# A four-layer transformer stack on one core: modulation pieces one unit later, the angle table inside a feed-forward stage, the closing x update shared with GpSimd, output by feature halves

## The chip, the cores and the metric

One core of one Trainium2 chip runs the whole program. Its engines are TensorE (PE, with its weight loads PEld), VectorE (DVE), ScalarE (ACT), GpSimd (POOL) and the sync engine's DMA queue (SP). The metric is the device time of one execution in microseconds. Everything is float32.

## The reference

x is 512 positions by 1024 features. Two blocks follow each other, each with two layers. A layer of the first block is a mixing part and a gated feed-forward part; a layer of the second block is a hybrid mixer and a feed-forward part with squared ReLU:

```python
for l in range(DEPTH):                                   # first block
    mod = c_act @ w_mod[l] + b_mod[l]                    # six vectors of 1024
    sh1, sc1, g1, sh2, sc2, g2 = split(mod)
    h = _rms(x, ln1[l]) * (1 + sc1) + sh1
    x = x + g1 * _mixing(h, ...)                         # top-k, stick-breaking and window attention
    h = _rms(x, ln2[l]) * (1 + sc2) + sh2
    x = x + g2 * ((silu(h @ w_gate) * (h @ w_up)) @ w_down)
for l in range(DEPTH):                                   # second block
    mod = cond @ w_ada[l] + b_ada[l]
    h = rmsnorm(x, norm_g[l, 0]) * (1 + sc_m) + sh_m
    y = hybrid(h, cos, sin, ...)                         # differential attention, latent attention, state scan
    x = x + g_m * rmsnorm(y, norm_g[l, 1])
    h = rmsnorm(x, norm_g[l, 2]) * (1 + sc_f) + sh_f
    y = square(relu(h @ w_up)) @ w_down
    x = x + g_f * rmsnorm(y, norm_g[l, 3])
```

cos and sin of the second block come from an input of positions, so the kernel computes that table of angles itself.

## The kernel before

**Layout.** x is kept in SBUF turned, as `xT`: eight tiles of 128 features by 512 positions. `hT` holds the normalized input. Weights come in slabs of up to 2 MB through a ring of two slots, `ring`; the sync queue issues slab n when the last product on slab n - 2 is done. Products go to eight PSUM banks.

**Order.** There is no scheduler. `order1(l)` and `order2(l)` write out one list of steps for each layer (`STEPS1`, `STEPS2`), and every engine walks the same list and does its part of each step, with semaphores between the parts. So a step's place in the list sets its place in the queue of each engine that has a part in it. `woven(*streams)` merges streams of steps: each is given a start and an end on a common scale, its steps are spread evenly between, and all are sorted by that position.

**Feed-forward stages.** `FFN1` has 38 units, `FFN2` 32. A unit is one product of two-by-two block form with seven part products (L1037): "gu" units make the hidden tiles, "dn" units the output, where two units (the second closes) make one result. Two units share a slab. For each unit GpSimd forms sums of weight blocks (`slab_sums`, step "S", L928 to L933, four additions, two units ahead), ScalarE copies the first product (L1518), VectorE recombines the products (L1998 to L2010) and, in the second block, forms the block differences of the hidden tiles ("turn", L1969 to L1972). `first_pair` (L1082) does the first two units of a stage together.

**Modulation of the next layer.** It is computed within a feed-forward stage from 24 pieces of 256 columns. The step "ma" is VectorE's weighted sum over half a piece (`mod_sum`: one instruction of L1958 and three of L1960 each), "mm" is TensorE's sum over partitions (`mod_product`, L1022), "mb" adds the bias. `ffn_steps` puts ma 2t and 2t + 1 behind unit t, mm t - 1 behind unit t, and mb t - 2 ahead of it. The half pieces are loaded by the sync queue (L874) between the slabs (L882), as `pieces_behind` says; half piece p is issued only when the sum of p - 2 is done. This happens in three of the four feed-forward stages.

**Ends of layers.** The second block starts with the steps prep, ns, nh: VectorE prepares small vectors, ScalarE squares the eight tiles of x (L1767), TensorE sums them with a matrix of ones (L1325), ScalarE forms the root, VectorE and ScalarE make `hT` (L2358, L1776). Ahead of it, behind the last step of the first block, VectorE computes the angle table in 18 small instructions (L2268 to L2279) and ScalarE its sine (L1716). A layer of the second block ends with "ys" (ScalarE squares the output y, L1738, GpSimd adds the squares, L981), "post" (TensorE's sum, ScalarE's root) and the x update on VectorE: for each of eight tiles y = y * modG * rb (L2557), x = x + y (L2558). After the last layer TensorE turns x back (L1505), VectorE copies eight banks (L2563), and one transfer of 2 MB writes the output (L900):

```python
            pe.wait_ge(*s2["x"].after(DEPTH - 1, KT))
            for i in range(QT):
                for half in range(2):
                    b = 2 * i + half
                    pe.wait_ge(free[b], final[b])
                    for t in range(4):
                        mm = pe.transpose(bank[b][:, P * t:P * t + P], xT[:, 4 * half + t, P * i:P * i + P], ident)
```

**Woven stages.** In the first block the top-k selection is 48 rounds of two VectorE instructions (L2157, L2158), woven with projections ("pj", "proj", "pss", "rope") and with the eight window groups, whose last step but one, "on", is VectorE's normalization (L2254) and whose last, "ot", is TensorE's turn of the result (L1281). In the second block 32 scans (L2528) are woven with the projections, the rotations "kr" and "mqr" (TensorE L1365, VectorE L2372) and the outputs "y" (L1478); the gated norms "sn" (L1359) and the output projection "wo" are woven with the attention groups.

## Time and profile before

| what | value |
|---|---|
| median of 3 runs | 3379.56 us (3372.46 to 3388.6) |
| profiled execution | 3382.9 us, its span 3381.1 us |
| busy: PE, PEld | 3074.4 us (91%), 2214.9 us (66%) |
| busy: DVE, ACT, POOL | 1730.5 us (51%), 761.5 us (23%), 923.7 us (27%) |
| mean granted TensorE clock | 0.941 |
| read from memory | 300.6 MB, 90 GB/s over the span |
| chain that ended last | PE 75%, DVE 12%, ACT 5%, DMA 2%, POOL 2% |

In the rows further down a line of a timeline is start, length, engine, source line, operation, tiles, shapes and count; brackets give how long the engine was idle before it and what it waited for. Merged lines of TensorE count each float32 product twice.

### The profile page before, as it was taken

The numbers are of one execution on the slowest core, as the hardware profiler recorded it, in microseconds if no ns is written. First come the engines' busy times: TensorE is split into PE (matmuls) and PEld (weight loads), VectorE is DVE, ScalarE is ACT, GpSimd is POOL, SyncE is SP. The second block draws the span as 40 slices with busy tenths as digits, with TensorE's granted clock in tenths as the row PEclk, the third lists the DMA queues.
The fourth block names the chain that finished last, engine by engine and source line by source line (L and its number), as shares of the span: only waits on it lengthen the run. The fifth ranks groups of instructions, "written<-read, shape, count | busy, mean of one in ns | idle before, by whom it ended". The sixth has DMA issues, their size and how long they took to land.

```text
span 3381.1 us, 34673 instructions
## 1 busy us (share of the span) xinstructions
PE 3074.4 (91%) x12632; PEld 2214.9 (66%) x12632; DVE 1730.5 (51%) x3718; ACT 761.5 (23%) x1781; POOL 923.7 (27%) x796
## 2 busy tenths in 40 slices
PE   6988989999998798999979988799997998899996
PEld 3444568888744467888854355688883435588885
DVE  1384337785328644877542633775724353452333
ACT  2234420000123542000022243310202234320110
POOL 0220023344312012344410400343440120234442
PEclk8997899999999889999989989899998998899998
DMA  5113214442211002445121111244421010122221
GB/s 203 62 39 146 79 63 162 172 169 98 95 50 50 25 13 93 165 155 196 62 77 45 34 49 38 87 150 185 164 100 46 33 50 26 50 75 75 100 75 50
DMA packets 38553, 304.97 MB, mean 90 GB/s; under 512 B 4192, under 2 KB 4320, under 8 KB 24176
## 3 DMA queue, kind: packets, MB, share of 16 engines
q1 hardware_dynamic: 38352, 302.68, 24.6%
q8 instruction: 103, 1.69, 0.2%
q14 instruction: 66, 0.54, 0.1%
q0 software_dynamic: 32, 0.07, 0.0%
HBM read 300.63 MB, written 2.10 MB: 90 GB/s over the span
## 4 chain that ended last, share of the span: by engine, by line
PE 75%; DVE 12%; ACT 5%; issue 3%; DMA 2%; POOL 2%; DVEq 0%; SPq 0%; POOLq 0%; ACTq 0%
PE bank L1037 41%; PE bank L1015 9%; PE bank L1345 7%; PE bank L1166 3%; PE bank L1082 3%; DMA ring<-in_slabs 2%; DVE nw L1960 1%; DVE sel L2158 1%; PE bank L1216 1%; DVE m L2157 1%; PE bank L1478 1%; PE bank L1153 1%; DVE SPT L2222 1%; PE bank L1203 1%; PE bank L1325 1%
## 5 line engine op out<-in xcount | busy, mean ns | idle before, releaser
L928 POOL TENSOR_TENSOR SPT<-ring 128x512 f32<-128x512 f32 (+2 forms) x140 | 170.4, 1217 | 1023.7 <-DMA ring<-in_slabs 501.9
L1037 PE MATMUL bank<-U,ring 128*128 128x256 f32 x1728 | 406.5, 380 | 0.3 <-DMA ring<-in_slabs 0.3
L1037 PEld LDWEIGHTS bank<-U,ring 128*128 128x128 f32 x1728 | 326.3, 190 | 43.6 <-DMA ring<-in_slabs 0.4
L1960 DVE SCALAR_TENSOR_TENSOR nw<-sel,c,nw 128x256 f32<-128x256 f32 x504 | 321.3, 638 | 40.3 <-DMA sel<-in_mod_pieces 22.7
L1037 PE MATMUL bank<-U,SPT 128*128 128x256 f32 x1296 | 311.4, 379 | 4.9 <-POOL SPT L933 4.9
L1037 PEld LDWEIGHTS bank<-U,SPT 128*128 128x128 f32 x1296 | 246.0, 190 | 39.4 <-POOL SPT L933 6.1
L1037 PE MATMUL bank<-hT,SPT 128*128 128x256 f32 x1088 | 257.0, 379 | 0.0
L1037 PE MATMUL bank<-hT,ring 128*128 128x256 f32 x1088 | 256.1, 389 | 0.3 <-DMA ring<-in_slabs 0.3
L1345 PE MATMUL bank<-hT,ring 128*128 128x512 f32 x544 | 246.0, 597 | 6.5 <-ACT hT L1776 6.5
L1166 PE MATMUL bank<-hT,ring 128*128 128x512 f32 x512 | 243.9, 620 | 5.0 <-ACT hT L1559 3.2
L1998 DVE TENSOR_TENSOR rb<-bank,nw 128x256 f32<-128x256 f32 x108 | 45.8, 424 | 375.8 <-PE bank L1037 286.4
L1037 PEld LDWEIGHTS bank<-hT,ring 128*128 128x128 f32 x1088 | 207.8, 195 | 27.9 <-DMA ring<-in_slabs 0.3
L1037 PEld LDWEIGHTS bank<-hT,SPT 128*128 128x128 f32 x1088 | 206.7, 190 | 28.1
L1518 ACT ACTIVATE nw<-bank 128x256 f32<-128x256 f32 x108 | 40.7, 377 | 759.4 <-PE bank L1037 759.0
L931 POOL TENSOR_TENSOR SPT<-SPT,ring 128x512 f32<-128x512 f32 (+2 forms) x140 | 190.1, 1358 | 0.0
L1015 PE MATMUL bank<-U,ring 128*128 128x512 f32 (+2 forms) x416 | 185.8, 588 | 0.0
L1345 PEld LDWEIGHTS bank<-hT,ring 128*128 128x128 f32 x544 | 99.8, 190 | 127.1 <-issue 124.1
L1166 PEld LDWEIGHTS bank<-hT,ring 128*128 128x128 f32 x512 | 99.0, 199 | 126.5 <-issue 124.5
L930 POOL TENSOR_TENSOR ring<-ring 128x512 f32<-128x512 f32 (+2 forms) x140 | 176.6, 1261 | 11.0
L933 POOL TENSOR_TENSOR SPT<-ring,SPT 128x512 f32<-128x512 f32 (+2 forms) x140 | 173.8, 1241 | 11.0
L990 POOL TENSOR_TENSOR SPT<-SPT,U 128x512 f32<-128x512 f32 (+3 forms) x48 | 55.9, 1190 | 332.2 <-DVE SPT L2528 332.2
L1015 PEld LDWEIGHTS bank<-U,ring 128*128 128x128 f32 (+1 forms) x416 | 84.1, 210 | 79.9 <-issue 76.6
(328 smaller groups left out, 4735.8 us busy)
## 6 DMA issues: line engine op xcount, KB each, us to landing
ring<-in_slabs SPq DMA_DIRECT2D x88, 2048.0 KB, 8.1
sel<-in_mod_pieces SPq DMA_DIRECT2D x144, 512.0 KB, 4.8
ring<-in_slabs SPq DMA_DIRECT2D x8, 1536.0 KB, 9.0
ring<-in_slabs SPq DMA_DIRECT2D x8, 1280.0 KB, 5.9
ring<-in_slabs SPq DMA_DIRECT2D x2, 2080.0 KB, 8.2
ring<-in_slabs SPq DMA_DIRECT2D x2, 1808.0 KB, 7.7
ring<-in_slabs SPq DMA_DIRECT2D x2, 1664.0 KB, 7.3
cst<-in_consts SPq DMA_DIRECT2D x1, 2120.0 KB, 23.7
```

The lines of the kernel that those rows point to most:

```text
L928: pool.tensor_tensor(e1, a21, a22, ALU.add).then_inc(*pool_order.up())
L930: pool.tensor_tensor(a21, a11, a21, ALU.subtract).then_inc(*pool_order.up())
L931: pool.tensor_tensor(e2, e1, a11, ALU.subtract).then_inc(*pool_order.up())
L933: pool.tensor_tensor(e4, a12, e2, ALU.subtract).then_inc(*s["sx"].up())
L990: pool.tensor_tensor(x, x, flat_x[:, g + tri[s]:g + tri[s + 1]], ALU.mult).then_inc(*s2["m"].up())
L1015: mm = pe.matmul(dst, lhs(k), rhs(k), start=(k == 0), stop=(k == n - 1))
L1037: mm = pe.matmul(into[j][:, c:c + HALF], lhs[:, k, :], rhs[:, k, :], start=(begin and k == 0), stop=(end and k == kp - 1))
L1082: mm = pe.matmul(bank[b][:, c:c + HALF], lhs[:, k, :], rhs[:, k, :], start=(k == 0), stop=(k == KT // 2 - 1))
L1166: mm = pe.matmul(bank[b][:, :], w8[:, k, P * col:P * col + P], hT[:, k, :], start=(k == 0), stop=(k == KT - 1))
L1345: mm = pe.matmul(bank[b][:, :], w[:, k, c:c + P], hT[:, k, :], start=(k == 0), stop=(k == KT - 1))
L1960: ins = dve.scalar_tensor_tensor(a, w[:, k, :], c[:, j:j + 1], a, ALU.mult, ALU.add)
L1998: link(dve.tensor_tensor(sum2, b[1][:, 0:HALF], first[set_turn(bk, u)], ALU.add))
```

## The change

Modulation: each ma, mm and mb step comes one unit later, and the half pieces are dealt to the slabs with none behind the first slab and four behind each later one (before: two and then four). The angle table becomes a step inside the feed-forward stage of the last layer of the first block, behind its unit 31; it works in tiles `sqb` and `yB` in place of `SPT`, and is else the same (its instructions are not shown). In the second block the squares of x become a step of their own, nq, ahead of prep. The closing x update is split: ScalarE multiplies y by modG (step yg, behind the squares), VectorE updates tiles 0, 1, 3, 4 and 6, GpSimd tiles 2, 5 and 7. The output is turned, copied (first half by ScalarE, second by VectorE) and written by halves of the features. Five weaves have other starts and ends.

```diff
+X_DVE, X_POOL = (0, 1, 3, 4, 6), (2, 5, 7)
...
     for t, u in enumerate(units):
-        if mods and 0 <= t - 2 < PIECES:
-            o.append(("mb", t - 2, at[t - 2]))
+        if mods and 0 <= t - 3 < PIECES:
+            o.append(("mb", t - 3, at[t - 3]))
         o.append(("unit",) + u)
...
         if mods:
-            if t < PIECES:
-                o += [("ma", 2 * t), ("ma", 2 * t + 1)]
             if 0 <= t - 1 < PIECES:
-                at[t - 1] = 4 * ((turn + 1) % 2)
-                o.append(("mm", t - 1, at[t - 1]))
+                o += [("ma", 2 * t - 2), ("ma", 2 * t - 1)]
+            if 0 <= t - 2 < PIECES:
+                at[t - 2] = 4 * ((turn + 1) % 2)
+                o.append(("mm", t - 2, at[t - 2]))
...
-    o += woven((0, 0.92, dense), (0.37, 1, group_slots(range(NC1))),
-               (0, 1, rounds + [[("seldone", i)] for i in range(1, QT)]))
+    o += woven((-0.03, 0.92, dense), (0.37, 1.01, group_slots(range(NC1))),
+               (0, 1.15, rounds + [[("seldone", i)] for i in range(1, QT)]))
...
-    o += woven((0, 0.95, stick_slots()), (0.08, 0.95, group_slots(range(NC1, len(GROUPS1)))),
+    o += woven((0, 0.96, stick_slots()), (0.08, 0.95, group_slots(range(NC1, len(GROUPS1)))),
...
-    o += ffn_steps(FFN1, 2, True, lambda t: [])
+    o += ffn_steps(FFN1, 2, True, lambda t: [("angles",)] if (l, t) == (DEPTH - 1, len(FFN1) - 7) else [])
...
 def order2(l):
-    o = [("prep",), ("ns", 0), ("nh", 0)]
+    o = [("nq",), ("prep",), ("ns", 0), ("nh", 0)]
...
-    o += woven((0, 1.04, dense), (0.1, 1, scans))
+    o += woven((0.03, 1.1, dense), (0.1, 0.93, scans))
...
-    o += woven((0.01, 1, keys), (-0.15, 0.4, [[("sz",)], [("sn", 0)], [("sn", 1)]]),
-               (0.09, 1, [c for slot in slots[:NM2] for c in slot]))
-    o += woven((0.2, 1, [[("wo", 0, n)] for n in range(KT)]), (-0.08, 1, [c for slot in slots[NM2:] for c in slot]))
+    o += woven((0.01, 1, keys), (-0.15, 0.53, [[("sz",)], [("sn", 0)], [("sn", 1)]]),
+               (0.1, 1, [c for slot in slots[:NM2] for c in slot]))
+    o += woven((0.25, 1, [[("wo", 0, n)] for n in range(KT)]), (-0.15, 1.07, [c for slot in slots[NM2:] for c in slot]))
...
-        return [("ys", 1, 2 * u[2]), ("ys", 1, 2 * u[2] + 1)] if u[0] == "dn" and u[1] == 1 and u[3] == 1 else []
+        return [(s, 1, n) for s in ("ys", "yg") for n in (2 * u[2], 2 * u[2] + 1)] if u[0] == "dn" and u[1] == 1 and u[3] == 1 else []
...
-    o += [("ys", 1, KT - 2), ("ys", 1, KT - 1), ("post", 1)]
+    o += [(s, 1, n) for s in ("ys", "yg") for n in (KT - 2, KT - 1)] + [("post", 1)]
...
     for n, key in enumerate(slabs):
-        out[key] = list(range(q, min(4 * n + 2, 2 * PIECES)))
-        q = min(4 * n + 2, 2 * PIECES)
+        out[key] = list(range(q, min(4 * n, 2 * PIECES)))
+        q = min(4 * n, 2 * PIECES)
...
+        def x_ready(l, k):
+            return s2["xp"].after(l, X_POOL.index(k) + 1) if k in X_POOL else s2["x"].after(l, X_DVE.index(k) + 1)
...
-            sp.wait_ge(out_ready, QT)
-            sp.dma_start(out[0].rearrange("(t p) d -> p t d", p=P),
-                         U[:, 0:8, :].rearrange("p (t a) n -> p t (a n)", t=QT)).then_inc(out_done, 16)
-            sp.wait_ge(out_done, 16)
+            for half in range(2):
+                sp.wait_ge(out_ready[half], QT)
+                sp.dma_start(out[0].rearrange("(t p) (a n) -> p t a n", p=P, a=2)[:, :, half, :],
+                             U[:, 0:8, :].rearrange("p (t a) n -> p t a n", a=2)[:, :, half, :]).then_inc(out_done, 16)
+            sp.wait_ge(out_done, 32)
...
+                pool.wait_ge(*s2["rstd"].after(l, 6))
+                pool.wait_ge(*s2["yg"].after(l, KT))
+                for n in X_POOL:
+                    y = y_tile(n)
+                    pool_link(pool.tensor_tensor(y, y, rb[:, 1, :], ALU.mult))
+                    pool.tensor_tensor(xT[:, n, :], xT[:, n, :], y, ALU.add).then_inc(*s2["xp"].up())
...
-            pe.wait_ge(*s2["x"].after(DEPTH - 1, KT))
-            for i in range(QT):
-                for half in range(2):
+            for half in range(2):
+                for t in range(4):
+                    pe.wait_ge(*x_ready(DEPTH - 1, 4 * half + t))
+                for i in range(QT):
                     b = 2 * i + half
...
+                    elif kind == "nq":
+                        for k in range(KT):
+                            act.wait_ge(*(x_ready(l - 1, k) if l else s1["xd"].after(DEPTH - 1, k // 2 + 1)))
+                            act.activation(hT[:, k, :], xT[:, k, :], ACT.Square).then_inc(*s2["sq"].up())
...
                     elif kind == "ns":
-                        if st[1] == 0:
-                            for k in range(KT):
-                                act.wait_ge(*s2["x"].after(l, k + 1 - KT))
-                                act.activation(hT[:, k, :], xT[:, k, :], ACT.Square).then_inc(*s2["sq"].up())
...
+                    elif kind == "yg":
+                        n = st[2]
+                        act.wait_ge(*s2["psq"].after(l, NS2 + 2 * KT + n + 1))
+                        act.activation(y_tile(n), y_tile(n), ACT.Copy, scale=modG[:, 1, n:n + 1]).then_inc(*s2["yg"].up())
...
+            for i in range(QT):
+                b = 2 * i
+                act.wait_ge(full[b], final[b] + 1)
+                act.activation(U[:, b, :], bank[b][:, :], ACT.Copy).then_inc(out_ready[0], 1)
...
                         dve.wait_ge(*s2["rstd"].after(l, 6))
-                        for n in range(KT):
+                        dve.wait_ge(*s2["yg"].after(l, KT))
+                        for n in X_DVE:
                             y = y_tile(n)
-                            link(dve.scalar_tensor_tensor(y, y, modG[:, 1, n:n + 1], rb[:, 1, :], ALU.mult, ALU.mult))
+                            link(dve.tensor_tensor(y, y, rb[:, 1, :], ALU.mult))
                             dve.tensor_tensor(xT[:, n, :], xT[:, n, :], y, ALU.add).then_inc(*s2["x"].up())
             for i in range(QT):
-                for half in range(2):
-                    b = 2 * i + half
-                    dve.wait_ge(full[b], final[b] + 1)
-                    ins = dve.tensor_copy(U[:, b, :], bank[b][:, :])
-                ins.then_inc(out_ready, 1)
+                b = 2 * i + 1
+                dve.wait_ge(full[b], final[b] + 1)
+                dve.tensor_copy(U[:, b, :], bank[b][:, :]).then_inc(out_ready[1], 1)
```

## Rows read from the trace of the kernel before

**Rows 1.** windows by stage: start:end, length, busy us per engine, clock, DMA share, GB/s.

```profile
124.00:436.00 312.00, 272.12 (x1103) 148.47 (x1102) 173.72 (x485) 121.06 (x315) 48.45 (x59) 0.87 0.21 75
...
505.00:905.00 400.00, 389.23 (x1832) 341.81 (x1832) 267.64 (x494) 28.42 (x56) 167.16 (x139) 0.99 0.40 142
...
980.00:1264.00 284.00, 241.67 (x906) 135.28 (x904) 173.77 (x475) 115.32 (x306) 49.27 (x59) 0.87 0.06 23
...
1860.00:2085.00 225.00, 202.02 (x674) 100.13 (x674) 109.14 (x281) 83.43 (x241) 36.73 (x32) 0.90 0.09 31
```

**Rows 2.** waits of TensorE, 500 to 905 us: total, times, longest.

```profile
PE bank L1022 <- DVE nw L1960: 8.0, 1, 8.0
```

**Rows 3.** chain that ended last, in time: start, length, units behind the waits.

```profile
510.69 14.13 PE bank L1037 x56
...
525.16 12.19 PE bank L1037 x56
...
1338.24 15.06 PE bank L1037 x56
...
2173.80 13.72 PE bank L1037 x56
```

**Rows 4.** timeline of VectorE, GpSimd and sync queue, first units.

```profile
503.24 6.32 DVE L1960 SCALAR_TENSOR_TENSOR nw<-sel,c,nw 128x256 f32<-128x256 f32 x7
...
513.75 0.35 DVE L1958 TENSOR_SCALAR nw<-sel,c 128x256 f32<-128x256 f32 x1
...
2177.64 3.61 DVE L1960 SCALAR_TENSOR_TENSOR nw<-sel,c,nw 128x256 f32<-128x256 f32 x7
...
518.15 0.43 SPq L882 DMA_DIRECT2D ring<-in_slabs  x1
...
528.35 1.45 POOL L928 TENSOR_TENSOR SPT<-ring 128x512 f32<-128x512 f32 x1 [21.16 <-DMA ring<-in_slabs]
```

**Rows 5.** timeline before the second block, all engines.

```profile
1700.63 0.42 DVE L1998 TENSOR_TENSOR rb<-bank,nw 128x256 f32<-128x256 f32 x1 [9.29 <-PE bank L1037]
...
1735.12 0.75 DVE L2100 SCALAR_TENSOR_TENSOR xT<-rb,modT,xT 128x512 f32<-128x512 f32 x1
...
1745.69 1.05 ACT L1716 ACTIVATE tab<-tab 32x1024 f32<-32x1024 f32 x1 [15.85 <-DVE tab L2279]
...
1750.31 8.70 PE L1325 MATMUL bank<-hT,cst 128*128 128x512 f32 x16 [17.01 <-ACT hT L1767]
```

**Rows 6.** timeline between the two layers of the second block.

```profile
2557.59 0.75 DVE L2557 SCALAR_TENSOR_TENSOR U<-U,modG,rb 128x512 f32<-128x512 f32 x1 [7.09 <-ACT rb L1746]
...
2568.10 0.69 DVE L2558 TENSOR_TENSOR xT<-xT,yB 128x512 f32<-128x512 f32 x1
...
2571.77 9.27 PE L1325 MATMUL bank<-hT,cst 128*128 128x512 f32 x16 [15.66 <-ACT hT L1767]
```

**Rows 7.** timeline, VectorE and GpSimd, late feed-forward units.

```profile
3300.08 1.75 DVE L2325 TENSOR_TENSOR U<-U,rb 128x512 f32<-128x512 f32 x1
...
3301.24 1.71 POOL L931 TENSOR_TENSOR SPT<-SPT,ring 128x512 f32<-128x512 f32 x1
...
3311.76 1.26 POOL L930 TENSOR_TENSOR ring<-ring 128x512 f32<-128x512 f32 x1
```

**Rows 8.** timeline of the tail, and the transfers' median time to landing.

```profile
3367.05 5.83 PE L1505 MATMUL bank<-cst,xT 128*128 128x128 f32 x32 [12.74 <-DVE xT L2558]
...
3374.13 0.40 SPq L900 DMA_DIRECT2D out_x<-U  x1
...
sel<-in_mod_pieces SPq DMA_DIRECT2D x144, 512.0 KB, 4.8
```

**Rows 9.** timeline of TensorE in woven stages, waits in brackets.

```profile
1143.51 0.66 PE L1281 MATMUL bank<-cst,SPT 128*128 128x128 f32 x2 [3.37 <-DVE SPT L2254]
...
1928.22 1.88 PE L1365 MATMUL bank<-U,cst 32*32 32x512 f32 x2 [3.30 <-DVE nw L2372]
...
1958.43 3.59 PE L1359 MATMUL bank<-sqb,cst 128*128 128x512 f32 x4 [2.49 <-ACT sqb L1738]
```

More of the change, by code:

```diff
@@ L2083, in _ @@
                         turn_first(l, s1)
+                    elif kind == "angles":
+                        dve.wait_ge(pos_in, 16)
+                        rows = slice(64, 96)
+                        pf, turns, ang = sqb[rows, 0, :], sqb[rows, 1, :], yB[rows, 0, :]
+                        link(dve.tensor_copy(pf, posi[rows, :]))
+                        link(dve.tensor_scalar(ang, pf, cst[rows, C_MISC + 4:C_MISC + 5], None, ALU.mult))
+                        for t, quarter in ((0, 0.25), (1, 0.0)):
+                            a = tab[rows, t, :]
+                            link(dve.tensor_scalar(turns, ang, 1.0 / TWO_PI, quarter, ALU.mult, ALU.add))
+                            link(dve.tensor_scalar(turns, turns, ROUND, None, ALU.add))
+                            link(dve.tensor_scalar(turns, turns, ROUND, None, ALU.subtract))
+                            link(dve.scalar_tensor_tensor(a, turns, -PI_A, ang, ALU.mult, ALU.add))
+                            link(dve.scalar_tensor_tensor(a, turns, -PI_B, a, ALU.mult, ALU.add))
+                            link(dve.scalar_tensor_tensor(a, turns, -PI_C, a, ALU.mult, ALU.add))
+                            link(dve.tensor_scalar(a, a, quarter * TWO_PI, PI_MAX, ALU.add, ALU.min))
+                            ins = dve.tensor_scalar(a, a, -PI_MAX, None, ALU.max)
+                            if t == 0:
+                                link(ins)
+                        ins.then_inc(pos_ready, 1)
                     elif kind == "unit" and closes(st[1:]):
```

31 lines of the change are left out of this document (6 added, 25 removed).

## The prediction

> **What bounds the kernel now.** I read the profile from the coarse views to the fine ones. First the windows by stage. In a feed-forward stage (505 to 905 us and the like) TensorE is busy 389 of 400 us at nearly full clock; in the two attention stages of the first block it idles 40 and 42 us, in the scan and attention stages of the second block 23 us, and a little over 24 in the second such layer, which repeats the row [rows 1]. So TensorE sets the time nearly everywhere, and only three things can be won: an idle stretch of TensorE, a low clock behind it, and the tail. Next the waits of TensorE in a feed-forward stage: one wait of 8.0 us for VectorE's weighted sums (L1960) [rows 2], most of the 11 us that are not busy. It comes three times, in every feed-forward stage that carries modulation pieces. Then the timeline at the three places where a layer ends: 17.0 us of idle before the second block [rows 5], some 15.7 between its two layers [rows 6], and a closing chain of x update, transposes, copies and one output transfer [rows 8]. All of these are touched by the diff.
>
> **Modulation one unit later.** Now mm 0 stands after unit 1 and needs ma 0 and 1, which VectorE begins only when unit 0 is recombined (503.24 less the 1.29 of its first instruction). They end at 509.6, and TensorE, done with the first pair at 509.7 - 8.0 = 501.7, waits [rows 2, 4]. After the change mm 0 stands behind unit 2, so TensorE goes straight into 12.2 us of products and asks at 513.9. VectorE first recombines unit 1 and does its two gate products, which in the trace take 4.2 us (from the end of the last sum at 509.56 to 513.75), and longer here, since GpSimd is adding just then: I take until 508.5. Then come two pieces, 4.0 us when GpSimd is quiet against 7.6 beside it [rows 4]: 512.5, so 1.4 us in hand. In the second block a turn of unit 0 stands in between, some 5 us while GpSimd still adds, so the pieces end near 13.6 us after the pair and mm 0 waits about 1.4. That gives 8.0 + 8.0 + 6.7 = 22.7 us. The clock adds to it: the unit behind the wait took 14.13, 15.06 and 13.72 us where an undisturbed one takes 12.19 [rows 3], so without the pause 1.9 + 2.9 + 1.5 = 6.3 us come back. The bound above is 24.1 + 6.3, the bound below nothing of the 6.3 and 5 us of new waits.
>
> What is late next: the sync queue issues slab 2 behind the pieces, and the last piece in front of it waits for the second sum before it. Today slab 2 is issued at 518.15, GpSimd begins on it at 528.35 and needs 5.4 us, against a demand at 510.56 + 25.1 + 3.5 = 539.1 [rows 3, 4]: 5 us in hand. Afterwards it is issued when ma 1 is done (512.7), its sums end at 528.4, and TensorE asks at 501.7 + 25.1 + 3.5 = 530.3: 1.9 us in hand. From there each piece, slab and unit stands to the others as before, since the split of pieces over slabs moves by two pieces as the sums move by one unit. Putting the first two pieces behind slab 1 costs nothing: they are wanted 30 us after that issue. At the end one more unit carries two pieces; VectorE, busy 268 of 400 us [rows 1], hides them.
>
> **Angle table.** Today VectorE ends the x update at 1735.87, then does 18 small instructions, ScalarE the sine and table loads, and only then come small preparations and the squares; TensorE ends at 1733.3 and starts the norm sum at 1750.31, taking 8.7 us to 1759.0 at a partly low clock [rows 5]. After: the squares of the first six tiles run during the last unit, TensorE takes their products at 1733.4 (8 at the full-clock price of about 0.86 us each, against 1.09 now), the last two squares (0.53 each) end by 1737.2, and the sum ends at about 1740.3. Gain 18.7 us. The table itself (9.8 us on VectorE, then some 3.6 on ScalarE) goes into a gap of 9.3 us between two recombinations [rows 5]. The sine delays ScalarE's copy for unit 33, so that recombination comes about 4 us late; its banks are wanted only four units on (15 us later), so this is hidden. Without that cover it would cost at most those 4 us.
>
> **Closing x update, middle.** Today 16 instructions on VectorE, 2557.59 to 2568.79 (11.2 us), then 2 us of preparations, squares and norm sum until 2581.0 [rows 6]. After: 10 tensor-tensor instructions on VectorE beside 6 on GpSimd. Alone they cost 0.69 and 1.26 us, but where both engines read SBUF together VectorE's took 1.75 and GpSimd's 1.71 [rows 7]. So GpSimd needs 6 x 1.7 = 10.2 us, VectorE gets 6 done in that time and 4 more at 0.69: the last x comes at 13.0, later than the 11.2 of today. What is won is order: squares and products follow tile by tile, the preparations no longer stand in front, and after the last x there are only two squares and two products, 2.7 us. The sum ends at 15.7 after 2557.6, that is 2573.3, gain 7.7. Without any contention it would be 13; with the two engines strictly in turn 10 x 0.69 + 6 x 1.26 = 14.5, gain 6.2. The Trainium skill ("SBUF — State Buffer", Who interferes with whom) says just that: an instruction of VectorE with two SBUF inputs and a GpSimd instruction that reads SBUF exclude one another. The rows agree in direction, and by its strict form my sum would be 1.5 us less at each of the two places. The eight scalings by modG that ScalarE takes over (about 0.6 each) lie under the last units or before the root, which waits for GpSimd's additions anyway.
>
> **The tail.** x takes the same 11.2 us, then transposes from 3367.05, the output is issued at 3374.13 and the span ends 7.0 later: 25.3 in all [rows 8]. After: tiles 0 to 3 are ready at 10.2, half the transposes cost 2.9, ScalarE's last copy ends at 13.8, and the first megabyte goes at 13.9. The second half: transposes 13.1 to 16.0, copy to 16.8. For 1 MB the bounds are half of 7.0 and all of it; a piece of 0.5 MB lands in 4.8 [rows 8], so I take 4.8 here too, the write being the quicker of the two. End at 21.7, gain 3.6; bounds -0.5 and 8.
>
> **Weave.** Of the moved steps one has a clear effect. In the first block the top-k rounds are spread wider, so about four of them (1.5 us each) fall behind the last group's normalization instead of ahead of it. TensorE waits 3.4 us for that instruction [rows 9]; VectorE idles after its rounds until the next stage has its first scores, so they have room. Gain 3.4 in each layer, 6.8. In the second block the scans are packed earlier and the two gated norms later: waits of 3.3 and 2.5 us are in their places [rows 9], but rotations and scans may collide anew. I take 2 of these 5.8 per layer, 4.0. Bounds for the whole weave: all of the waits named and as much again of the 82 us of idle in the first block (+24), and the same waits doubled instead of removed (-13).
>
> **Sum.** 22.7 + 6.3 + 18.7 + 7.7 + 3.6 + 6.8 + 4.0 = 69.8 us. The profiled execution took 3382.9 us (span 3381.1 and 1.8 around it); the median of the runs is 3379.6. Against the median: 3309.8, forecast 3310. Under 0.5% (17 us) a measurement of this kernel can hardly tell from no change.
>
> **Rivals.** *The wait moves to the slab sums.* The 1.9 us in hand at slab 2 turn into waits for GpSimd in each stage, and with the low clock after them only some 8 of the 29 us stay: 3331. For it: the margin is thin. Against: the order from there on is unchanged. Chance 0.12. *The weave works against itself,* rotations of the second block waiting behind scans, top-k behind the stick stage: -13 in place of +11, 3334. Chance 0.10. *The weave and the tail give more:* waits named here draw shorter ones and low clock with them, +17: 3293. For it: TensorE's clock in these stages is 0.87 to 0.90 [rows 1]. Chance 0.15. *Slabs fall behind for good (slower).* TensorE is 8.9 us ahead at slab 2 and the issue only 5.5. If VectorE never makes up these 3.4 us and they recur at each of some 12 slabs that carry pieces, in three stages, from the point where the 1.9 in hand is used up, this costs 34 x 3.4 = 116 us: 3426. Against it: VectorE has 130 us free in such a stage. Chance 0.03. *The chain of the angle table is not the one that holds the second block* (something else, as a bank, releases the norm sum late): 19 less, 3329. Chance 0.05. My forecast, within 3300 and 3322, has 0.55. Leaving out the slower case and the far ends of the weave, the range is 3288 to 3336. Faster 0.95, same 0.03, slower 0.02.
>
> **What would show it.** The wait before the first modulation product gone, the next unit at 12.2 us; under 1 us of idle between the last unit and the norm sum of the second block; GpSimd and VectorE both near 1.7 us per instruction in the x update, with the last x about 13 us after its start; the output in two transfers; the 3.4 us wait for the last group gone. It would be wrong if waits for GpSimd's sums or for slabs grew in the feed-forward stages.

## The result, and the profile after

Beside each other on one chip the kernel before took 3376.46 us (median of 4 runs) and the changed one 3289.51 us (4 runs, 3286.83 to 3293.26): ratio 0.9731, 95% interval 0.9709 to 0.9753. The gain is 87 us where 70 were forecast: the time lies below the 3300 to 3322 us of the forecast and just inside its outer limits of 3288 and 3336. Five more runs of the changed kernel, again beside the kernel before, gave 3291.08 us against 3380.32 (0.9741, 0.9717 to 0.9765); of all nine the middle one is 3290.8 us, and experiments below are set against it. The profiled execution took 3288.22 us, its span is 3286.2 against 3381.1.

The stages of the two profiled executions, cut at TensorE's first instruction of each part (us; the last two columns are a second trace of each kernel, from the experiments). "Attention" is everything from a layer's norm sum to its first pair of feed-forward units:

| part | before | changed | difference | before, 2nd | changed, 2nd |
|---|---|---|---|---|---|
| first block, attention, layer 0 | 438.7 | 424.4 | -14.3 | 434.2 | 426.6 |
| first pair | 42.9 | 32.4 | -10.5 | 41.2 | 32.6 |
| feed-forward | 394.7 | 398.0 | +3.3 | 394.3 | 398.1 |
| attention, layer 1 | 391.5 | 382.6 | -8.9 | 389.7 | 382.7 |
| first pair | 41.4 | 32.1 | -9.3 | 41.4 | 33.8 |
| feed-forward | 395.2 | 398.3 | +3.1 | 395.6 | 399.4 |
| pause before the second block | 17.0 | -0.2 | -17.2 | 17.0 | -0.2 |
| second block, attention, layer 0 | 371.4 | 357.5 | -13.9 | 368.1 | 361.8 |
| first pair | 52.0 | 42.2 | -9.8 | 51.7 | 42.1 |
| feed-forward | 374.6 | 375.3 | +0.7 | 374.6 | 375.5 |
| between its layers | 32.7 | 25.8 | -6.9 | 32.7 | 25.7 |
| attention, layer 1 | 359.7 | 352.2 | -7.5 | 359.7 | 352.1 |
| x update to the end | 34.6 | 31.4 | -3.2 | 34.6 | 31.4 |

In layer 1 of the second block attention begins at the end of the norm sum, which "between its layers" includes. "x update to the end" begins at the end of the last unit. A pause of -0.2 means that the norm sum starts before the modelled end of the last product. The last layer's first pair (43.0 and 42.1 us) and feed-forward stage (362.8 both times) are left out.

Nearly half of the fall (44.6 of 94.9 us) lies in the four attention stages, where my sum had 10.8 us for the weaves. The windows of these stages show of what it is made; first the kernel before (start:end, length, busy us of TensorE, its weight loads, VectorE, ScalarE and GpSimd, granted clock, DMA share, GB/s):

```profile
29.00:468.00 439.00, 391.08 (x1508) 215.62 (x1509) 193.73 (x526) 152.05 (x373) 62.54 (x70) 0.89 0.24 88
905.00:1297.00 392.00, 344.87 (x1222) 195.65 (x1221) 197.40 (x525) 142.42 (x357) 64.11 (x70) 0.90 0.11 40
1750.00:2122.00 372.00, 339.48 (x1106) 177.95 (x1106) 154.08 (x361) 127.17 (x328) 49.89 (x49) 0.94 0.12 44
2581.00:2941.00 360.00, 326.40 (x1090) 171.89 (x1090) 153.35 (x358) 123.01 (x320) 49.83 (x49) 0.95 0.12 42
```

The same view of the changed kernel, with its second feed-forward stage last:

```profile
29.00:454.00 425.00, 378.94 (x1508) 209.11 (x1509) 196.42 (x526) 152.14 (x374) 62.43 (x70) 0.91 0.24 89
884.00:1267.00 383.00, 338.51 (x1221) 192.09 (x1221) 199.39 (x525) 142.11 (x356) 63.64 (x70) 0.92 0.11 38
1697.00:2055.00 358.00, 331.80 (x1106) 175.45 (x1105) 158.72 (x379) 124.99 (x325) 49.32 (x49) 0.95 0.14 50
2498.00:2850.00 352.00, 324.77 (x1089) 172.06 (x1089) 153.12 (x358) 123.37 (x320) 48.87 (x48) 0.95 0.12 43
1299.00:1697.00 398.00, 389.06 (x1833) 341.31 (x1833) 285.20 (x515) 32.99 (x62) 170.38 (x141) 1.00 0.40 143
```

Length less busy time is what TensorE idles: 47.9, 47.1, 32.5 and 33.6 us before, 46.1, 44.5, 26.2 and 27.2 after, 17.1 us less. The number of matmuls is the same within one, yet they are busy 27.8 us less, at a granted clock one or two hundredths higher in three of the four stages (in the last it is 0.95 both times). In the feed-forward stage for comparison it is 1.00.

In this pair of traces more of the 45 us is clock than waiting, but that split doesn't repeat. The second pair's first stage, before and changed:

```profile
27.00:461.00 434.00, 385.94 (x1506) 214.62 (x1507) 193.51 (x525) 151.95 (x373) 62.73 (x70) 0.90 0.24 90
29.00:455.00 426.00, 381.38 (x1504) 208.51 (x1505) 195.04 (x525) 151.64 (x373) 62.52 (x70) 0.90 0.24 89
```

Over its four stages the second pair falls by 28.5 us, of which some 19 are idle time and 9 busy time. Over all traces of this document (first block: 7 with the old weaves against 10 with the new, second block: 6 against 12) the four stages fall by 39.6 us on average, 15.2 idle and 24.5 busy; about 1 us of the latter is a quicker norm sum. So the waiting part varies little, 15 to 19 us, and the clock part is anything from 9 to 28.

The waits of TensorE in the changed kernel's feed-forward stage of layer 0, 481 to 884 us (us in total, times, longest):

```profile
PE bank L1049 <- POOL SPT L939: 4.1, 2, 2.1
PE bank L1049 <- DVE modN L2095: 2.9, 6, 0.7
PE bank L1034 <- DVE modN L2095: 1.4, 2, 0.9
...
```

The 8.0 us of [rows 2] are gone; small waits for `mb` came in (4.3 us against 1.2), and those for GpSimd's sums stayed (4.1 against 4.5). In the second trace of the changed kernel the latter grew, to 6.4 us in layer 0 and 4.9 in layer 1, from 3.8 in each in the second trace of before. In the second block the whole stage has 1.1 us for the pieces (I had 1.4) and 0.2 for GpSimd, against one wait of 8.1. The timelines of VectorE and TensorE at the first product show why:

```profile
490.29 1.76 DVE L2131 TENSOR_TENSOR U<-U,rb 128x512 f32<-128x512 f32 x1
...
492.68 0.35 DVE L1977 TENSOR_SCALAR nw<-sel,c 128x256 f32<-128x256 f32 x1
493.07 3.61 DVE L1979 SCALAR_TENSOR_TENSOR nw<-sel,c,nw 128x256 f32<-128x256 f32 x7
...
498.10 0.50 PE L1034 MATMUL bank<-cst,nw 128*128 128x1 f32 x4
...
515.82 6.34 DVE L1979 SCALAR_TENSOR_TENSOR nw<-sel,c,nw 128x256 f32<-128x256 f32 x7
...
524.22 3.69 PE L1049 MATMUL bank<-hT,ring 128*128 128x256 f32 x16 [0.55 <-DVE modN L2095]
```

The pieces begin at 492.68 and end at 496.7, with 1.4 us in hand as worked out, and there is no wait in brackets at 498.10. But in the next odd unit the same two pieces take 7.6 us (515.82 and the 1.24 before it), because GpSimd is adding then, and TensorE's next unit waits 0.55 us for `mb`.

The start of the second block, all engines, in the changed kernel (answers to [rows 5]):

```profile
1668.99 1.05 ACT L1729 ACTIVATE tab<-tab 32x1024 f32<-32x1024 f32 x1 [20.63 <-DVE tab L2118]
...
1671.36 0.38 ACT L1530 ACTIVATE nw<-bank 128x256 f32<-128x256 f32 x1
1671.77 0.42 DVE L2017 TENSOR_TENSOR rb<-bank,nw 128x256 f32<-128x256 f32 x1 [2.81 <-ACT nw L1530]
...
1693.70 3.23 ACT L1773 ACTIVATE hT<-xT 128x512 f32<-128x512 f32 x6
...
1696.98 7.03 PE L1337 MATMUL bank<-hT,cst 128*128 128x512 f32 x16
```

No bracket stands behind 1696.98: the norm sum follows the last unit without a pause, and the late sine holds back one recombination by 2.81 us, which nobody waits for. The x update between the layers of the second block (answers to [rows 6, 7]):

```profile
2481.25 1.26 POOL L1008 TENSOR_TENSOR U<-U,rb 128x512 f32<-128x512 f32 x1 [3.66 <-ACT rb L1758]
2481.26 1.80 DVE L2577 TENSOR_TENSOR U<-U,rb 128x512 f32<-128x512 f32 x1 [7.08 <-ACT rb L1758]
...
2483.09 1.63 DVE L2578 TENSOR_TENSOR xT<-xT,U 128x512 f32<-128x512 f32 x1
2484.14 1.71 POOL L1008 TENSOR_TENSOR yB<-yB,rb 128x512 f32<-128x512 f32 x1
...
2487.48 1.72 POOL L1008 TENSOR_TENSOR yB<-yB,rb 128x512 f32<-128x512 f32 x1
...
2491.34 0.68 DVE L2577 TENSOR_TENSOR yB<-yB,rb 128x512 f32<-128x512 f32 x1
...
2493.38 0.69 DVE L2578 TENSOR_TENSOR xT<-xT,yB 128x512 f32<-128x512 f32 x1
2494.11 1.15 ACT L1773 ACTIVATE hT<-xT 128x512 f32<-128x512 f32 x2 [0.18 <-DVE xT L2578]
```

As forecast: about 1.7 us each while both engines run, 0.69 when VectorE is alone, the last x 12.8 us after the start (13.0 forecast). The tail (answers to [rows 8]):

```profile
3274.49 6.08 PE L1518 MATMUL bank<-cst,xT 128*128 128x128 f32 x32 [11.87 <-DVE xT L2578]
...
3278.80 3.25 SPq L906 DMA_DIRECT2D out_x<-U  x2
3279.03 2.59 DVE L2582 COPY U<-bank 128x512 f32<-128x512 f32 x4 [2.13 <-PE bank L1518]
```

From the start of the update at 3264.08 to the end of the span it is 22.1 us (21.7 forecast, 25.3 before).

### The profile page after: what moved, and what is told of

It reads as the page before. It is cut to its first block, busy times and chain, and to the rows that moved or that the text cites. A ratio compares the mean times of both kernels' runs of the same rounds, so it can differ in the third digit from the quotient of the medians.

```text
span 3286.2 us, 34698 instructions
## 1 busy us (share of the span) xinstructions
PE 3042.8 (93%) x12632; PEld 2198.4 (67%) x12632; DVE 1740.7 (53%) x3702; ACT 773.7 (24%) x1801; POOL 941.5 (29%) x808
## 3 DMA queue, kind: packets, MB, share of 16 engines
q8 instruction: 102, 1.67, 0.2%
## 4 chain that ended last, share of the span: by engine, by line
PE 73%; DVE 14%; ACT 5%; issue 3%; DMA 3%; POOL 2%; DVEq 0%; SPq 0%; ACTq 0%; POOLq 0%
PE bank L1049 39%; PE bank L1027 9%; PE bank L1357 7%; PE bank L1094 3%; PE bank L1178 3%; DVE nw L1979 2%; DMA ring<-in_slabs 2%; DVE sel L2196 1%; PE bank L1490 1%; DVE m L2195 1%; PE bank L1228 1%; DVE SPT L2260 1%; PE bank L1165 1%; ACT SPT L1675 1%; PE bank L1215 1%
## 5 line engine op out<-in xcount | busy, mean ns | idle before, releaser
L1027 PE MATMUL bank<-U,ring 128*128 128x512 f32 (+2 forms) x416 | 176.7, 564 | 0.0
L1049 PE MATMUL bank<-VT,SPT 128*128 128x256 f32 x544 | 130.4, 383 | 2.5 <-POOL SPT L939 2.5
```

What stands on the lines that cost most here:

```text
L1027: mm = pe.matmul(dst, lhs(k), rhs(k), start=(k == 0), stop=(k == n - 1))
L1049: mm = pe.matmul(into[j][:, c:c + HALF], lhs[:, k, :], rhs[:, k, :], start=(begin and k == 0), stop=(end and k == kp - 1))
```

## The experiments

There are eighteen runs; four of them repeat a kernel for a second trace or more timed runs. For those with the changed kernel as base, the difference is to 3290.8 us; for those with the kernel before as base, to 3379.86, its median beside them (22 runs).

**Which part gives more than forecast.** The changed kernel with all five weaves as before:

```diff
-    o += woven((-0.03, 0.92, dense), (0.37, 1.01, group_slots(range(NC1))),
-               (0, 1.15, rounds + [[("seldone", i)] for i in range(1, QT)]))
+    o += woven((0, 0.92, dense), (0.37, 1, group_slots(range(NC1))),
+               (0, 1, rounds + [[("seldone", i)] for i in range(1, QT)]))
...
-    o += woven((0.03, 1.1, dense), (0.1, 0.93, scans))
+    o += woven((0, 1.04, dense), (0.1, 1, scans))
...
```

> The kernel after the change with the five weaves of before. Theory W (the stages between the trace milestones are right: the weaves gave 14.1 + 8.8 + 13.8 + 9.2 = 45.9 us of the 94.9 us that the span fell): slower than the changed kernel by about 46 us, so some 3335 us, ratio to before near 0.987. Rival P (my prediction was right on the weaves, and the rest of the time in those stages is a clock that TensorE is granted by chance in one profile): slower than the changed kernel by 11 us only, some 3300 us, ratio near 0.977.

Measured: 3334.72 us, 44 us slower, near theory W. In the four attention stages TensorE idles some 12 us more than in the two traces of the changed kernel and is busy 29 to 37 us more. The kernel before with the modulation shift alone, with the first block's weaves alone, and with the second block's weaves alone:

> The kernel before with only the modulation one unit later and the half pieces dealt accordingly. Theory: 21 us faster, as the milestones of the full change show (7.1 + 6.2 + 7.7), with new waits of under 1 us for VectorE's bias step every second unit; ratio 0.994. Rival (the prediction): 29 us faster, ratio 0.991.

> The kernel before with only the first block's weaves of after. Theory W: 22.9 us faster, of which TensorE's busy time falls by some 19 (its clock) and its waits by only 4. Rival P: 6.8 us faster, all of it one wait of 3.4 us in each layer.

> The kernel before with only the second block's weaves of after. Theory W: 23 us faster, half from waits (idle in the stage 23 to 15.6 us in each layer), half from TensorE's busy time. Rival P: 4 us faster.

Measured: 3365.5 (ratio 0.9964, 0.9945 to 0.9984), 3369.35 (0.9975, 0.9959 to 0.999) and 3358.43 us (0.9941, 0.9919 to 0.9962), so 14, 11 and 21 us. The first two expectations missed (21 or 29, and 22.9 or 6.8), the third held (23). The weaves are worth 44 us in the full change and 32 when each half is done alone; the modulation gives only half of its 29. In the trace of the shift alone the three first pairs take 32.2, 32.5 and 43.1 us, a gain of 28.5; what is missing went elsewhere: 4.7 us in the feed-forward stages, the rest below.

**Parts undone in the changed kernel.** First the scan weave, then the key and output weaves of the second block:

> The changed kernel, with the weave of the scans (second block, decayed scans among the dense tiles) as it was before and all else as changed. Theory A (the gain of the second block's weaves lies in the scan weave, where most of the small waits for yB and the mixing matrices stood): the stage from the first norm sum of the second block to its feed-forward part, 357.5 us in the changed kernel, goes back to about 369, and the one of the other layer from 352.2 to about 361; the whole kernel is about 20 us slower than the changed one. Theory B (it lies in the key and output projection weaves with the gated norms): under 4 us in each stage, under 8 in all.

> The changed kernel, with the two later weaves of the second block (key tiles with the gated norms, output projection with the attention slots) as before and all else as changed. Theory A: under 4 us in each of the two stages, the whole under 8 us slower than the changed kernel. Theory B: about 10 to 12 us in each stage and 20 or more in all. If neither alone gives the 23 us by which the two stages together fell, the parts are not additive and the clock behind the waits is shared.

Measured: 3297.63 and 3304.93 us, 7 and 14 us slower; the stages of the second block are 362.7 and 355.5 us in the one, 364.5 and 354.8 in the other, so neither theory A nor B held. Both parts seem to give something, and the two medians add up to the 21 us that the same weaves gave alone. But each is near the scatter: the eleven traces of the changed kernel and of its variants that keep these weaves have 357.5 to 362.1 and 352.1 to 354.9 us in these stages. The waits of TensorE in the second block's first stage, 1697 to 2055 us, in the changed kernel:

```profile
PE bank L1457 <- ACT yB L1856: 3.8, 4, 1.8
...
PE bank L1371 <- ACT sqb L1750: 1.7, 1, 1.7
...
PE bank L1377 <- DVE nw L2391: 1.1, 1, 1.1
```

and the same lines with the scan weave undone, then with the two later weaves undone:

```profile
PE bank L1457 <- ACT yB L1856: 3.8, 4, 1.8
PE bank L1377 <- DVE nw L2391: 3.3, 1, 3.3
...
PE bank L1371 <- ACT sqb L1750: 1.7, 1, 1.7
```

```profile
PE bank L1457 <- ACT yB L1856: 5.5, 4, 3.1
...
PE bank L1371 <- ACT sqb L1750: 2.5, 1, 2.5
...
PE bank L1377 <- DVE nw L2391: 1.1, 1, 1.1
```

The 3.3 us wait of [rows 9] belongs to the scan weave. The later two shorten the waits for `yB` and for the squares (2.5 us); the prediction had counted the second and not the first, four waits that were 7.1 us in all before. Other waits take most of that back: with the later two undone TensorE's idle time in the two stages is 27.0 and 24.6 us, against 26.2 and 27.2, and what is lost is busy time (6.2 and 5.5 us).

The first block's weaves undone, then only the end of the top-k rounds (1.15 back to 1):

> The changed kernel with the two weaves of the first block as before, all else as changed. If the parts add up, the two stages of the first block are 10 and 5 us longer, mostly as TensorE busy time at a lower clock (granted clock of the first stage 0.89 in place of 0.91), and the kernel some 15 us slower, 3305. If the first block's weave is worth no more than my sum had (6.8 us, all of it waiting time), 3296 and the busy time of TensorE in these stages unchanged within 2 us.

> The changed kernel with the top-k rounds ending at 1 and not at 1.15 of the weave, all else as changed. My prediction put the whole gain of the first block's weaves on this one number (3.4 us in each layer, the wait for the last group's normalization): then the kernel is 6.8 us slower and each of the two stages 3.4 us longer. Rival: since that wait is still there in the changed kernel (4.2 us), the rounds are not what sets it, and undoing them changes each stage by under 1 us of waiting time; what else changes is clock.

Measured: 3307.14 us (16 slower, the stages 438.3 and 388.2 us) and 3296.3 us (5.5 slower, 431.0 and 389.9). So the rounds' end is worth about what the sum had for it (6.8), but not by the wait that it named. That wait, for the normalization of the last groups (L1293), stands in the changed kernel at 4.2 us in both layers (3.5 and 3.4 before); in layer 0:

```profile
280.08 0.66 PE L1293 MATMUL bank<-cst,SPT 128*128 128x128 f32 x2 [1.15 <-DVE SPT L2292]
284.96 0.66 PE L1293 MATMUL bank<-cst,SPT 128*128 128x128 f32 x2 [4.21 <-DVE SPT L2292]
```

With the rounds' end undone it is 3.0 us, not longer; TensorE idles some 2 us more in each stage, and the rest of the difference is its busy time. Neither expectation, 3.4 us or under 1 us of waiting per stage, was met.

**The modulation shift undone in the changed kernel.**

```diff
-        if mods and 0 <= t - 3 < PIECES:
-            o.append(("mb", t - 3, at[t - 3]))
+        if mods and 0 <= t - 2 < PIECES:
+            o.append(("mb", t - 2, at[t - 2]))
...
```

> The changed kernel with the modulation pieces one unit earlier again, as before, and all else as changed. My sum: 22.7 us of waits and 6.3 of clock come back as a loss, 29 us, so about 3318 us. Rival N (net gain smaller: the waits of 8 us go, but TensorE's other waits, for the last pieces' additions and the slab sums, and the clock of the stages around take back half, since the shift alone gave only about 14 us in the timed runs): about 14 us, so about 3304. In either case the stretch from the first pair of units to the next is about 42 us in the first block and 52 in the second, against 32.4 and 42.2.

Measured: 3316.89 us, 26 us slower, and the first pairs take 41.6, 41.2 and 51.6 us again, while the feed-forward stages get 6.7 us shorter (394.9, 395.4 and 374.6). In the full change the term comes near what the sum had (29).

**The x update and the output.** All eight tiles on VectorE (`X_DVE = (0, ..., 7)`, `X_POOL = ()`), and one output transfer in place of two:

> The changed kernel, with all eight x tiles of the closing update on VectorE and none on GpSimd. Theory of the contention: 16 instructions at about 0.69 us end at 11.1 us after the start of the update, where the shared update ended at 12.8, since VectorE's instructions cost 1.6 to 1.8 us beside GpSimd's; so the norm sum between the layers of the second block ends 1 to 2 us earlier and the tail is 1.5 to 3 us shorter (tiles 0 to 3, and with them the first half of the output, come at 5.6 us instead of about 10); 3 to 5 us in all. Rival (sharing pays, the two engines overlap in part): the last x comes later than 12.8 us and both places lose 1 us or more.

> The changed kernel with one output transfer of 2 MB, issued when all copies are done, in place of two of 1 MB by feature halves. Theory of my sum (the landing time goes with the bytes, 7.0 us for 2 MB and less for 1): the tail from the start of the x update to the end, 22.1 us in the changed kernel, becomes about 24 us. Rival (a fixed share of the landing prevails and the first transfer only delays or does nothing): it stays within 0.7 us of 22.1.

Measured: with x on VectorE the 16 instructions take 0.69 us each and the last x comes 10.7 us after the start. The first and last of them between the layers, in that kernel:

```profile
2484.84 0.69 DVE L2577 TENSOR_TENSOR U<-U,rb 128x512 f32<-128x512 f32 x1 [7.08 <-ACT rb L1758]
...
2494.86 0.69 DVE L2578 TENSOR_TENSOR xT<-xT,yB 128x512 f32<-128x512 f32 x1
```

The stretch between the layers falls from 25.8 to 21.8 us and the last part from 31.4 to 28.3. So GpSimd's share costs 4 us in the middle and 3 at the end: what the change wins there, it wins by the order of squares and preparations and by the halves, in spite of the sharing. The median, 3288.86 us, did not show it, so both kernels ran again side by side. With one output transfer the median is 3290.6 us, the same as with two; only the trace tells them apart (below).

> The changed kernel once more, on the chip of the run beside it, for the comparison with x on VectorE. If its stages vary by clock alone, the waiting time of TensorE in each stage repeats within 1 us and the attention stages differ by up to 5 us from the first trace; median about 3290.

> The changed kernel with all x tiles of the closing update on VectorE. In the trace it won 4.0 us between the layers of the second block and 3.1 us at the end, while four timed runs showed nothing. If the 7 us are lasting and only the scatter of the clock hid them, the median is 5 to 9 us under that of the changed kernel beside it. If the clock gives back what the shorter pause between the layers wins, it is within 3 us of it, and the attention stage behind that pause is longer by about as much.

Measured: 3291.08 and 3283.14 us; ratios to before 0.9741 (0.9717 to 0.9765) and 0.9719 (0.9697 to 0.9742). The two intervals overlap, so the timed runs alone don't decide; the traces agree again (21.8 us between the layers, 29.9 in the last part). Between the layers the three traces with x on VectorE have 21.8 us and all with sharing 25.2 to 26.1; at the end the gain is 1.5 to 3 us. Of nine timed runs each the medians are 3287.2 and 3290.8. It has the lowest time here, by less than its traces show. The changed kernel's own second trace repeats TensorE's idle time in the attention stages within 1.5 us. With one output transfer the last part is 33.9 us, 24.7 from the start of the update, 2.6 more than with two, within 0.7 of the 24 expected: the theory of bytes, not of a fixed share, held. Each 1 MB transfer landed in 4.2 us.

**The angle table behind the last unit,** the step `("angles",)` at `len(FFN1) - 1` instead of `- 7`:

> The changed kernel with the angle table computed behind the last feed-forward unit of the first block, ahead of the squares, instead of seven units earlier. By my sum the table is on the path there: 9.8 us on VectorE, 1.1 of sine, 1.3 of table load and then the squares, so the first norm sum of the second block ends 13 to 15 us later than in the changed kernel, and the timed runs are 13 to 15 us slower, about 3304. Rival (such a pause is partly given back by what stands behind it): the norm sum is as late as that, but the next stage is shorter or the timed runs lose only half of it.

Measured: 3312.71 us, 22 slower. The norm sum in that kernel:

```profile
1711.82 1.05 ACT L1729 ACTIVATE tab<-tab 32x1024 f32<-32x1024 f32 x1 [15.85 <-DVE tab L2118]
...
1714.19 4.26 ACT L1773 ACTIVATE hT<-xT 128x512 f32<-128x512 f32 x8
1714.96 8.86 PE L1337 MATMUL bank<-hT,cst 128*128 128x512 f32 x16 [15.54 <-ACT hT L1773]
```

It starts 15.7 us later against the last unit and takes 8.86 us in place of 7.03: 17.5 in all, a little over my bound of 15; the 22 us of the timed runs hold 4 more, which I don't attribute. Nothing is given back; behind the pause TensorE is also slower for the sum itself.

**Where the clock goes.** The kernel before once more, and the modulation shift alone once more:

> The kernel before, unchanged, with a second trace. It shows how much a stage varies with the same order of steps. If the clock is what varies, the feed-forward stages agree within 1 us with the first trace, the waiting time of TensorE within 1 us everywhere, and the attention stages differ by 2 to 10 us in TensorE's busy time alone, with another granted clock. If the stages repeat within 1 us, the differences between traces of one order seen so far have another cause, such as the chip.

> The kernel before with the modulation shift alone, a second trace. Its first trace kept the 29.6 us at the three first pairs but lost 5 to 7 us in each attention stage of the second block, against both traces of the kernel before, with the same order of steps and a lower granted clock. Chance: the two stages come out anywhere between 368 and 375 and between 360 and 365. A lasting effect of where the modulation leaves the clock: 374.5 and 364.4 again within 0.5 us.

Measured: the kernel before differs from its first trace by 4.5, 1.8, 3.3 and 0.0 us in the four attention stages, with TensorE's idle time within 1.1 us of the first (48.1, 48.2, 31.6, 33.5): it is the clock that varies with one order of steps. The shift alone repeats 376.6 and 367.2 us in the second block's attention, after 374.5 and 364.4, where the kernel before has 371.4 and 368.1, and 359.7 twice. Both expectations missed: it is not within 0.5 us, but on the long side both times, and so are these stages (374.4 and 364.5) when everything but the weaves is changed. Against the two traces of before that is 11 us more on average, all of it TensorE busy time (granted clock 0.91 to 0.93 where before has 0.94 and 0.95), and most of the 14 us that are missing. But the first block's weaves alone, without the shift, lengthen them too (374.7 and 362.9), so it is not the shift as such. With the second block's new weaves, shift or no shift makes at most 4 us there (361.1 and 353.9 without it, 357.5 to 361.8 and 352.1 with it). Why the old ones lose there what was won further ahead, these runs don't show.

Then the two pauses of 1.2 and 4.2 us shown above filled, as far as it went, with idle transposes of the identity, and the rounds spread still further:

```diff
                         g = st[1]
+                        for _ in range({NC1 - 2: 3, NC1 - 1: 11}.get(g, 0)):
+                            pe.transpose(dst[:, 0:P], ident, ident)
                         pe.wait_ge(*s1["un"].after(l, g + 1))
```

> The changed kernel, with 14 idle transposes of the identity (3 and 11, of about 0.33 us each) on TensorE in front of its two waits of 1.2 and 4.2 us for the last groups' normalization in the first block; they write a bank that the real transposes overwrite, so nothing computed changes. Theory C (the low clock of TensorE behind these places, 0.67 to 0.98 of full over the next 80 us, comes from TensorE's pauses just before): the granted clock of these 80 us rises, TensorE's busy time in the stage falls by 2 us or more besides the fillers' own, and each of the two stages gets 2 to 6 us shorter. Theory D (the clock there goes by something else, and a filled pause saves nothing): the clock stays and the stage is as long as before or up to 1 us longer.

> The changed kernel with all x tiles on VectorE and the top-k rounds spread once more, to 1.3 of the weave instead of 1.15. From the run with x on VectorE: 4.1 us less between the layers of the second block and 3.1 us less at the end. If spreading the rounds has more to give: 3 us less in each stage of the first block (3276 in all). If 1.15 was already enough, the last rounds now stand in front of the next stage's scores and it is the same or 3 us worse per stage (3282 to 3290).

The 120 us from there on, one row for each kernel: the kernel before, its second trace, and the kernel with only the second block's weaves changed (its order in this stretch is that of before),

```profile
269.00:389.00 120.00, 103.40 (x483) 59.61 (x482) 43.75 (x141) 48.26 (x119) 8.45 (x20) 0.74 0.42 158
```

```profile
267.00:387.00 120.00, 103.27 (x510) 60.56 (x509) 47.68 (x149) 52.58 (x127) 8.46 (x20) 0.80 0.43 158
```

```profile
269.00:389.00 120.00, 102.56 (x532) 60.95 (x532) 48.43 (x150) 53.95 (x131) 10.13 (x24) 0.86 0.43 158
```

then the changed kernel, the one with filled pauses, and the one with the rounds to 1.3:

```profile
269.00:389.00 120.00, 104.01 (x549) 61.89 (x547) 54.49 (x157) 57.30 (x139) 10.14 (x24) 0.84 0.43 158
```

```profile
268.00:388.00 120.00, 107.03 (x557) 63.59 (x556) 54.38 (x164) 55.91 (x135) 10.16 (x24) 0.84 0.43 158
```

```profile
269.00:389.00 120.00, 104.30 (x475) 60.02 (x474) 53.12 (x153) 49.46 (x122) 8.47 (x20) 0.72 0.43 158
```

TensorE is busy 103 to 104 us of the 120 in all but the filled one; what differs is how much it does in them, 475 to 549 matmuls at 0.72 to 0.86. One order of steps gave 0.74, 0.80 and 0.86. The chip is not the reason: of the seven kernels with the old order in this stretch the three that ran on one chip have 0.74, 0.80 and 0.86 (all weaves undone, the shift alone, the second block's weaves alone). With the new order all eleven traces have 0.83 or 0.84. So the new order does not beat the old at its best, 427.2 us for the stage against 423.8 to 426.6; it was never seen in the old one's low clock.

Filling the pauses took 3 us of them and left the clock at 0.84: the stages came out at 425.9 and 380.8 us against 424.4 and 426.6, and 382.6 and 382.7, 3297.39 us in all. In layer 0 theory C, that these pauses set this low stretch, fell and D held. In layer 1 the transposes ran out with 2.3 us of the longer pause left; the clock of the 80 us behind it is 0.79 against 0.78, and the stage is the shortest of its kind by 1.2 us, which doesn't stand out of the scatter. The rounds to 1.3 lost the whole gain of the first stage (437.8 us, 3297.93 in all, in spite of x on VectorE), more than either expectation had.

## Why the prediction was right or wrong

**Modulation, 22.7 + 6.3: mechanism right, 26 us when undone.** The wait of 8 us went, mm 0 had 1.4 us in hand, slab 2 was in time. The three first pairs alone gave 29.6 (25.8 in the second pair of traces); 7 us of it (8.5) went in the feed-forward stages, mostly in waits: in the profiled execution those for `mb` grew by 3.1 us in layer 0 and 1.4 in layer 1, where 1.5 us more for a slab's transfer came with them. I had new waits in the lower bound alone. In the second pair it was the waits for GpSimd's sums that grew, by 2.6 and 1.1 us: the thin margin of the first rival and my own sign of being wrong, seen there in a small form. I had the doubled price of pieces beside GpSimd in hand [rows 4], but used it only for the first pair of pieces.

**Angle table and norm sum, 18.7: measured 17.2 of pause and 1.7 of a quicker sum, 18.9.** The chain was the one that held the second block.

**Middle x update 7.7, tail 3.6: measured 6.9 and 3.2.** The contention term was near (12.8 us for 13.0). The Trainium skill ("SBUF — State Buffer", Who interferes with whom) says that two-input VectorE instructions and GpSimd's SBUF reads exclude each other. Here one instruction of each took some 1.67 us together (two of each between 2484.14 and 2487.48), where strict turns would be 0.69 + 1.26 = 1.95; strict turns would have given 14.5 us for the update. The direction holds, the strict sum doesn't.

**The weaves, 6.8 + 4.0: the step that failed.** Measured 44 us by undoing them, 44.6 by the four stages of the profiled executions (1.7 of it the quicker norm sum above), 28.5 by those of the second pair, 39.6 on average of all traces. Three things in it were wrong. It counted one named wait in the first block and two in the second and took the rest for nothing: idle time fell by 4.4 us in the first block, less than the 6.8 of the sum, and by 12.7 in the second, where the sum had 4.0. It named the wrong wait in the first block: the 3.4 us became 4.2, and the stage got shorter all the same. And, the largest part, it priced waiting time alone, though the same prediction had added a clock term behind the modulation wait and its own rows gave these stages 0.87 to 0.90: busy time fell by 27.8 us more in the profiled pair, 9 in the second, 24.5 on average. The upper bound of +24 was made from named waits too, and so stood under the measured value. It is also not what its words give: with the second block's 5.8 us in each of two layers, as the sum counts them, the named waits are 18.4 us and the bounds about +37 and -18, and +37 still lies under most of what was measured. The rival "the weave and the tail give more" (3293) had the direction and some of the mechanism, clock with the waits; its +17 was half of the 33 us by which the weaves went over. That the total came out only 17 us over is in part luck: the feed-forward stages gave back 7 and the two x updates 1, and the medians fell by 8 us less than the profiled pair (87 against 94.9).

What sets the clock in these stretches stays open. In layer 0 it is not the two filled pauses. It is not the order of steps alone, since one order gave 0.74 to 0.86, and not the chip. That the weaves shift the average is seen in all traces: with the new first-block weaves, the first stage took 423.8 to 426.6 us in all eleven traces of kernels that have them (431.0 and 437.8 with the rounds' end at 1 and at 1.3); with the old ones it took 427.2 to 438.7 in seven. The other three stages part in the same way: 380.8 to 386.8 against 388.2 to 392.6, 357.5 to 362.1 against 368.1 to 376.6, 350.5 to 354.9 against 359.7 to 367.2 (traces in which a weave of just that stage is undone or moved further are left out).

## What to carry to other kernels

In a stage where TensorE idles and its granted clock is low (here 9 to 12% and 0.89 to 0.95), price a reordering by the stage's idle and clock together, not by the one or two waits that can be named: here 12 to 19 us of idle came with 9 to 37 of busy time at another clock. Judge such a change by several traces of each order, since the same order differs by up to 11.5 us in a stage. Sharing elementwise work on SBUF tensors between VectorE and GpSimd can cost more than it takes away: 16 instructions on one engine took 10.7 us, on two 12.8.

## What the runs showed of the hardware

With one order of steps the first attention stage took 427.2, 434.2 and 438.7 us and its 120 us from 269 on had a granted clock of 0.86, 0.80 and 0.74; TensorE's idle time there stayed at 48 us. With the new order that stretch had 0.83 or 0.84 in eleven traces. TensorE's norm sum of 16 matmuls took 7.03 us straight behind a unit and 8.86 behind a pause of 15.5. A VectorE tensor-tensor of 128x512 took 0.69 us alone and 1.63 to 1.80 beside GpSimd's, which took 1.26 alone and 1.59 to 1.72; the first of GpSimd's, started 0.01 us ahead of VectorE's, took 1.26 all the same. An output of 1 MB landed in 4.2 us, one of 2 MB in 6.6.
